# A two-layer encoder trunk on one core: the first mixer's attention rebuilt head by head

## The reference

```python
proj = x @ w_in
q, k, v, u = jnp.split(proj, ...)            # 8 query heads, 2 key/value heads of 64; u: 2 x 512 channels
q = apply_rope(rms_norm(q, q_norm_g), cos, sin)
k = apply_rope(rms_norm(k, k_norm_g), cos, sin)
# attention, each query head against all 512 keys of its group of 4
s = jnp.einsum('bqkgd,bskd->bkgqs', q_blk, k) * 64 ** -0.5
o = jnp.einsum('bkgqs,bskd->bqkgd', softmax(s), v)
# conformer convolution
a, gate = jnp.split(u, 2, axis=-1)
z = a * sigmoid(gate)                         # GLU, 512 channels
z = depthwise_conv(z, width 31) + dw_b        # over the tokens, per channel
conv = silu(layer_norm(z, norm_g, norm_b))    # norm over channels
m = concatenate([attn, conv]) @ w_out
```

## Time and profile before

| | us |
|---|---|
| median of 3 runs | 1436.73 (1434.38 to 1438.51) |
| the profiled execution | 1434.18 |
| its span | 1432.4 |
| PE busy in the span | 1383.2 (97%) |
| DVE busy | 664.6 (46%) |
| ACT busy | 459.6 (32%) |
| POOL busy | 221.6 (15%) |
| start of the output projection of layer 0 | 224.42 |

### The profile page before, as it was taken

One profiled execution on the slowest core, in us unless ns is written; L12 is line 12 of the kernel. 1 busy time (PEld: TensorE's weight loads), 2 busy tenths in 40 slices (PEclk: granted clock), 3 DMA queues, 4 the chain that ended last, 5 costly groups with the idle time before them and its releaser, 6 DMA issues.

```text
span 1432.4 us, 16564 instructions
## 1 busy us (share of the span) xinstructions
PE 1383.2 (97%) x6684; PEld 1162.5 (81%) x6684; DVE 664.6 (46%) x823; ACT 459.6 (32%) x552; POOL 221.6 (15%) x194
## 2 busy tenths in 40 slices
PE   7969789999999999999999999999999999999997
PEld 7757677888888888889888888888888888888886
DVE  4669893733333322166555453654373333332225
ACT  3357553332232221133232332423233222322211
POOL 5279851300000000033201002000030000000000
PEclk9989999999999999999999999999999999999999
DMA  6200001223222332303231212222222233224221
GB/s 213 89 30 1 30 30 59 89 88 109 96 88 94 109 120 88 115 33 137 67 105 59 88 59 88 89 89 89 88 89 88 88 99 106 88 89 146 88 89 59
DMA packets 84015, 124.15 MB, mean 87 GB/s; under 512 B 2688, under 2 KB 61312, under 8 KB 83968
## 3 DMA queue, kind: packets, MB, share of 16 engines
q1 hardware_dynamic: 83968, 123.49, 25.7%
HBM read 121.39 MB, written 2.10 MB: 86 GB/s over the span
## 4 chain that ended last, share of the span: by engine, by line
PE 86%; DVE 6%; POOL 4%; ACT 2%; issue 1%; DMA 0%; POOLq 0%; DVEq 0%; SPq 0%; ACTq 0%
PE ps L1236 22%; PE ps L1238 22%; PE ps L1237 22%; PE ps L1312 19%; DVE acc L914 2%; POOL acc L501 2%; POOL w_lo L377 1%; PE ps L1249 1%; ACT w_hi L373 1%; DVE row_max L1000 1%; DVE probT_lo L1017 1%; PE ps L1522 0%; PE ps L1442 0%; DMA x_tok<-in_x 0%; DVE x_tok L1059 0%
## 5 line engine op out<-in xcount | busy, mean ns | idle before, releaser
L377 DVE TENSOR_TENSOR w_lo<-raw,w_hi 128x2048 fp32r<-128x2048 f32 x101 | 231.8, 2295 | 487.1 <-ACT w_hi L373 487.1
L1236 PE MATMUL ps<-xT_hi,w_hi 128*128 128x512 f32 (+1 forms) x992 | 366.6, 370 | 0.5 <-POOL w_lo L377 0.5
L1237 PE MATMUL ps<-xT_lo,w_hi 128*128 128x512 f32 (+1 forms) x992 | 365.5, 368 | 0.0
L1238 PE MATMUL ps<-xT_hi,w_lo 128*128 128x512 f32 (+1 forms) x992 | 365.5, 368 | 0.0
L373 ACT ACTIVATE w_hi<-raw 128x2048 fp32r<-128x2048 f32 x109 | 208.4, 1912 | 429.7 <-PE ps L1238 251.1
L1236 PEld LDWEIGHTS ps<-xT_hi,w_hi 128*128 128x128 f32 x992 | 186.9, 188 | 32.1 <-POOL w_lo L377 1.1
L1238 PEld LDWEIGHTS ps<-xT_hi,w_lo 128*128 128x128 f32 x992 | 186.9, 188 | 31.4
L1237 PEld LDWEIGHTS ps<-xT_lo,w_hi 128*128 128x128 f32 x992 | 187.0, 188 | 31.2
L575 POOL TENSOR_SCALAR var_eps<-var_eps 128x1 f32<-128x1 f32 x16 | 5.6, 352 | 846.9 <-ACT squares L768 846.9
L1236 PE MATMUL ps<-w_hi,xT_hi 128*128 128x512 f32 (+1 forms) x320 | 121.3, 379 | 0.0
L1237 PE MATMUL ps<-w_lo,xT_hi 128*128 128x512 f32 (+1 forms) x320 | 121.1, 378 | 0.0
(11 more groups left out here) (167 smaller groups left out, 1760.8 us busy)
## 6 DMA issues: line engine op xcount, KB each, us to landing
raw<-in_l_w_in SPq DMA_DIRECT2D x31, 1024.0 KB, 5.2
raw<-in_l_ffn_w_gate SPq DMA_DIRECT2D x22, 1024.0 KB, 5.1
raw<-in_l_ffn_w_up SPq DMA_DIRECT2D x22, 1024.0 KB, 5.1
raw<-in_l_ffn_w_down SPq DMA_DIRECT2D x22, 1024.0 KB, 4.7
raw<-in_l_w_out SPq DMA_DIRECT2D x12, 1024.0 KB, 4.9
x_tok<-in_x SPq DMA_DIRECT2D x4, 512.0 KB, 7.2
out<-x_tok SPq DMA_DIRECT2D x8, 256.0 KB, 2.1
ln_gb<-in_l_ln_mix_g SPq DMA_DIRECT2D x2, 512.0 KB, 5.2
```

Of the source, the lines that this page charges most:

```text
L377: eng.tensor_tensor(w_lo[ch.s][:], raw[ch.s][:], f32(w_hi[ch.s][:]), ALU.subtract)\
L1236: nc.tensor.matmul(dst, a[0], b[0], start=start, stop=False)
L1237: nc.tensor.matmul(dst, a[0], b[1], start=False, stop=False)
L1238: return nc.tensor.matmul(dst, a[1], b[0], start=False, stop=stop)
```

## The change

- **Order of the head.** The first GLU pair is multiplied ahead of the queries: chunks are now KV, GLU 0 gate, GLU 0 value, Q, Q, GLU 1 gate, GLU 1 value, and each GLU pair is gate first.
- **Queries and keys.** The query is scaled by `q_scale` before it is turned and written twice side by side (`q_twice`, 1024 wide, line 998 of the new kernel, on DVE). After the turn, rows 0 to 63 hold its rounded part and rows 64 to 127 the rest (`q_pair`). The key stands twice and negated (`k_hi`, `k_lo`). One matmul over 128 rows thus does two parts, and the scores take two matmuls in place of three. They are the negative scores, and their row minimum is the exponential's shift: one DVE reduction (line 1020), with no `neg_max` behind it.
- **Order of the loop.** Step s is head s // 4, tile s % 4. The probabilities of one head are kept for all 512 queries, in two buffers.
- **Weighted values.** Once a head's four tiles are there, `weighted_values` issues 12 matmuls of 512 columns in one go (in steps 7, 11, ... 31 for the first seven heads, behind the last step for the eighth), with the output by feature. Two heads share a bank.
- **Division.** For a pair of heads POOL takes the inverse row sums and spreads them over 512 columns (`inv_wide`), PE turns them, ACT copies, DVE multiplies (`pair_scaled`) and takes the rest (`pair_lo`). `divide_outputs` and the turns of the output go.
- **Convolution.** All 31 taps of tile 3 are on PE, one each step (three matmuls). DVE has 46 taps in place of 49, 14 of them ahead of the loop, then one a step. POOL adds one a step.
- **Norm of the convolution.** It comes behind the loop. PE does the first two chunks' rows of token tiles 0 and 1 of the output projection in between (`first_rows`).

```diff
-C_Q = 1
-C_GLU = (3, 5)
+C_GLU = (1, 5)
+C_Q = 3
...
-            add_taps(18)
+            add_taps(7)
+            query_scale(0)
+            for t in range(1, TT):
+                add_taps(1)
+                query_scale(t)
...
+            add_taps(8)
...
             def attention_step(s):
-                b = s // 2
-                add_taps(1 + (s % 4 == 1))
+                b = s // 4
+                add_taps(1)
...
+            make_hi(act, Chunk(C_Q + 1))
+            tap_products(9)
             make_hi(act, Chunk(C_GLU[1]))
...
+            for t in range(TT):
+                query_square(t)
+                tap_products(1 + (t % 2))
             make_hi(act, Chunk(C_GLU[1] + 1))
-            glu_sigmoid(1)
-            tap_products(16)
+            tap_products(2)
             glu_sigmoid(2)
-            tap_products(4)
+            query_hi(0)
+            query_hi(1)
+            tap_products(2)
             glu_sigmoid(3)
...
-                mine(nc.vector.tensor_reduce(row_max[:, s:s + 1], ps[:, SCORE_BANKS[s % 2], :], AX.X, ALU.max))
-                nc.vector.tensor_scalar(neg_max[:, s:s + 1], row_max[:, s:s + 1], q_scale[:, t, h:h + 1], -1.0,
-                                        ALU.mult, ALU.mult).then_inc(max_made, 1)
...
+                nc.vector.tensor_reduce(neg_max[:, s:s + 1], ps[:, SCORE_BANKS[s % 2], :], AX.X, ALU.min).then_inc(max_made, 1)
...
-                conv(2 - s % 2)
...
+                conv(1)
+                if s >= 14 and s % 8 == 6 and s // 8 - 1 < PAIRS - 1:
+                    pair_scaled(s // 8 - 1)
+                if s >= 16 and s % 8 == 0 and s // 8 - 2 < PAIRS - 1:
+                    pair_lo(s // 8 - 2)
...
+                q, g = q_pair[:, t, h, :], h // (HEADS // KV)
+                nc.tensor.matmul(ps[:, SCORE_BANKS[s % 2], :], q, k_hi[:, g, :], start=True, stop=False)
+                nc.tensor.matmul(ps[:, SCORE_BANKS[s % 2], :], q, k_lo[:, g, :], start=False, stop=True).then_inc(scores_made, 1)
...
+                h, part = (s - 7) // TT, (s - 7) % TT
+                if 0 <= h < HEADS - 1 and part == 0:
+                    weighted_values(h, range(TT))
...
+            def weighted_values(h, key_tiles):
...
+                if 0 in key_tiles:
+                    pe.wait_ge(probT_lo_made, TT * (h + 1))
...
+                for k in key_tiles:
+                    v = v_parts[:, k, g].rearrange("p c d -> p (c d)")
+                    v_hi, v_lo = (v[:, HD * (c - odd):HD * (c - odd) + P] for c in (1, 3))
+                    last = product(out, (v_hi, v_lo), (probT_hi[:, b, k, :], probT_lo[:, b, k, :]),
+                                   not odd and k == 0, odd and k == TT - 1)
...
+            conv_to_tokens(0)
+            conv_to_tokens(1)
+            wait_split(pe, C_OUT0)
+            pe.wait_ge(att_lo_made, 2)
+            first_rows(0, 0)
+            conv_to_tokens(2)
+            pe.wait_ge(o_scaled, PAIRS - 1)
+            first_rows(0, 1)
+            conv_to_tokens(3)
+            wait_split(pe, C_OUT0 + 1)
+            pe.wait_ge(att_lo_made, PAIRS)
+            first_rows(1, 0)
+            first_rows(1, 1)
+            pe.wait_ge(conv_normed, TT)
+            for ct in range(CT):
+                conv_to_features(ct)
```

More of the change, by code:

```diff
@@ L407, in _ @@
                 sp.dma_start(dst, src).then_inc(par_landed, 16)
[L408 to L411, removed]
+            load(sp, Chunk(C_GLU[0] + 1), W0[:, :, A0:A0 + 256])
+            for j in range(2):
+                load(sp, Chunk(C_Q + j), W0[:, 4 * j:4 * j + 4, 0:512])
+            load_glu(1)
             for j in range(4):
@@ L553, in conv_rsqrt @@
                     .then_inc(conv_rstd, 1)
[L555 to L567, removed]
+            for s in range(LAST_STEP):
                 attention_step(s)
-            divide_outputs(STEPS // GROUP - 2)
-            conv_rsqrt(TT - 1)
-            divide_outputs(STEPS // GROUP - 1)
+            for t in range(TT):
+                conv_rsqrt(t)
             def norm_rstd(d, t):
@@ L1006, in _ @@
+            row_shift(0)
+            row_shift(1)
+            for n in range(TT, 2 * TT):
+                query_lo(n)
             glu_product(3)
@@ L1391, in glu_tiles @@
-            def glu_tiles(part, banks, between):
-                wait_split(pe, part)
-                feature_tiles(Chunk(part), banks, between)
-            glu_tiles(C_GLU[0], SIDE_B[0:2], lambda m: None)
-            pe.wait_ge(kT_lo_made, 4)
-            for t in range(2):
-                q_transposes(t)
-            glu_tiles(C_GLU[0] + 1, SIDE_B[2:4], lambda m: [q_transposes(t) for t in (2, 3)] if m else None)
-            glu_tiles(C_GLU[1], SIDE_B[0:2], lambda m: pe.wait_ge(z_made, m + 1))
@@ L1403, in attention_step @@
+            glu_tiles(C_GLU[1] + 1, VALUE_BANKS, inside_value)
             def attention_step(s):
@@ new lines, in _ @@
+            first_rows(0, 0)
[8 more added lines that the diff above has]
+            pe.wait_ge(conv_normed, TT)
+            for ct in range(CT):
+                conv_to_features(ct)
+            for t in (2, 3):
+                pe.wait_ge(silu_made, 2 * (t - 1))
+                last = first_rows(0, t)
@@ L1493, in swiglu @@
+            last.then_inc(chunk_used, 1)
+            for t in (2, 3):
+                last = first_rows(1, t)
+            last.then_inc(chunk_used, 1)
+            last_rows(C_OUT0, 4, (catT_hi, catT_lo), lambda row: pe.wait_ge(swish_lo_made, row - 3), 1)
             def swiglu(layer, c_ffn, c_down, stage):
```

562 lines of the change are left out of this document (301 added, 261 removed).

## The result

The changed kernel takes 1441.78 us (median of 6 runs, 1441.11 to 1443.21), the kernel before 1435.83 (6 runs): ratio 1.0041, 95% interval 1.0028 to 1.0054. It is slower by 0.4%, where 0.77% faster was forecast. The profiled execution took 1441.26 us.

The account below looks back on a forecast made before the run. DVE was taken to pace the loop, behind an 11 us hole on PE. Head -2.4, loop -8.7, tail 0 gave -11.1: span 1421.3, execution 1423, median 1425.6 us; own range 1418 to 1431, eight in ten 1415 to 1441.

Parts of the forecast that it names:

- that one moment: Mixer's end, where the output projection begins, 224.42 us before; gains were summed up to there, everything behind taken as unchanged.
- The loop: 29 steps, from step 2's reduction to step 31's: 93 us, 8.7 less than 101.7; range 87 to 106.
- I add 5 us: Loop: allowance for four queues waiting for each other, about one earlier DVE stall of 4.53 us.
- The sum of the parts: Loop without coupling: 25 steps at 2.70 us (67.5), splits 6, pair scalings 4.2, last four steps 9.6; 87.3 us.
- the burst by itself should be hidden: Loop: a head's twelve weighted-value products take 2.74 us, the scores behind wanted about 1.3 us later than they come.
- rival 3: Slower, chance 0.15: PE's low clock makes bursts 5.2 us and loop steps 2.1 longer; ten such steps give 1447.
- The head: Up to step 2's reduction: at about 109 us, 2.4 earlier than before; range 8 earlier to 8 later.
- The tail: From step 31's reduction to the mixer's end: 11.3 us net against 11.4 before, so no change; range 3 either way.
- Reductions that wait for PE after each burst: Loop, sign of being wrong: every fourth step longer than the others by more than 1 us.
- The signs of being right: Reductions 2.7 us apart in steps 3 to 26, step 2's near 109, step 31's near 202, PE idle below 6 before the loop.
- its 92: Head, sign of being wrong: the third sigmoid later than 92 us; it was expected near 87.5.
- the bound of 0.9: Loop, sign of being wrong: PE's granted clock below 0.9 over tens of us.

Follow-up runs that it names:

- e1_pad: The changed kernel with 128 unused bytes ahead of `work`, so its tensors stand where they stood before: 1433.25 us, 0.9978 of the kernel before.
- e2_before_moved: The kernel before with `row_max` placed elsewhere, so `work` and all behind it lies 128 bytes lower: 1443.9 us, 1.0057 of the kernel before.
- e5_inverse_later: The changed kernel with the transposes of a pair's inverse row sums two steps later, behind the burst, and ACT's copy one step later: 1430.45 us.
- e6_filled: The changed kernel with 28 extra products on PE ahead of its wait for the inverse of the first and second pair: 1439.07 us.
- e11_diagonals_first: The changed kernel with 128 bytes ahead of `work`, inverse transposes two steps later, and POOL's first two diagonal blocks ahead of its first seven additions: 1419.12 us.
- e3_split_late: The changed kernel with POOL's two splits of output weights in steps 13 and 21 instead of 8 and 16: 1439.57 us.
- e8_before_256: The kernel before with `row_max` and `neg_max` placed elsewhere, so `work` lies 256 bytes lower: 1436.38 us, 0.9996 of the kernel before.

## Why the prediction was wrong, step by step

**The sum left out a term: 8 us.** "Behind it nothing is changed, so the sum is made for that one moment": the code behind wasn't changed, its operands' addresses were. 7.17 us behind the mixer and 0.9 in the output projection; e1_pad and e2_before_moved show it in both directions, 8.5 and 7.2 us by the medians. It is more than twice the 3.4 us that the rebuilt mixer gains without it, and it alone turns the change from faster to slower. It is not the whole error: with the address put back the time is 1433.25 us, still above the forecast's own range of 1418 to 1431.

**The loop: 98.78 us instead of 93.** The term "I add 5 us" for coupling failed: DVE waits 19.78 us for scores. A second error of the other sign hides most of that. The sum of the parts, 87.3 us, was too large, for DVE is busy only 77.07 us in the loop (third pair of numbers, the columns of the earlier trace rows); of the changed kernel and of e5_inverse_later:

```profile
111.00:209.78 98.78, 73.51 (x345) 55.23 (x346) 77.07 (x93) 61.11 (x128) 70.26 (x48) 0.90 0.06 22
```

```profile
112.50:199.10 86.60, 69.95 (x345) 52.96 (x346) 74.54 (x93) 61.22 (x128) 72.91 (x48) 0.98 0.07 25
```

I had priced nearly every step at 2.70 us, with a tap beside POOL. Where POOL neither adds nor splits beside it, a tap has 0.73 us (139.78) and reductions come 1.87 apart (steps 8 and 9, 12 and 13, 20 and 21). That e5_inverse_later, without most of the waits for the inverse, comes to 86.60 and so near to 87.3 is chance: its DVE is busy 74.54 us and waits 10.4 for scores.

What made the coupling large: I had listed the inverses and the splits as load on POOL (81.5 against 87 us) and not as a queue: the inverse stands behind a 4.53 us split in POOL's order, and PE's place for it is *ahead* of the burst and of the next scores. The step "the burst by itself should be hidden ... about 1.3 us later than they come" was right for a burst without a wait ahead: 1.40 us at 127.46, at the full clock.

**The low clock (rival 3)** did not come as described, on step after step. It came behind the two long waits for the inverse and cost 2.7 us there (e6_filled). In e5_inverse_later, with the same change of banks from step to step and PE's short waits still there, the granted clock (behind PE's count) stays at its upper level until 160 us:

```profile
106.50:143.00 36.50, 27.40 (x136) 1.00 0.07 19
143.00:160.00 17.00, 12.70 (x68) 1.00 0.06 23
```

The Trainium skill (TensorE: Matmul & The Clock Gate, A second HAM failure mode) tells of a kernel whose clock swings because it cycles through PSUM banks; these two rows, 53.5 us of such a loop at 1.00, show no swing. Later in the same loop the clock did fall once, near 177 us, behind the wait of 1.98 us shown above. What let it fall there and not behind the 1.95 us at 150.31 is open.

**The head: step 2 at 111.00, not 109.** The order of events was right, and ACT's first tap came at 48.66 us (48.5 forecast); two sizes were not. ACT and POOL:

```profile
89.48 0.72 ACT L650 ACTIVATE tap_part<-zpad,conv_par 128x512 f32<-128x512 f32 x1 [10.24 <-POOL acc L499]
...
91.52 0.58 ACT L661 ACTIVATE tmp<-ps 128x512 f32<-128x512 f32 x1
```

```profile
82.44 1.65 POOL L512 TENSOR_TENSOR q_scale<-q_ms,minus_half 128x8 f32<-128x8 f32 x1 [5.77 <-DVE q_ms L992]
84.06 3.17 POOL L526 TENSOR_TENSOR diag<-ident,conv_par 128x512 f32<-128x512 f32 x2
```

The fourth scale came at 82.44 (79 assumed), since DVE ahead of it took 2.20 and 2.17 us for each wide scaling (1.5 assumed) and waited 1.51 for ACT's rounding of a weight chunk; two diagonals took 3.17 (2.5 assumed). So the third sigmoid starts at 91.52 and not near 87.5; of these 4 us 2.0 arrive at step 2. e11_diagonals_first, in which step 2 comes 2.0 us earlier, shows that the two diagonals lie on that path.

**The tail: +3.2 instead of nothing.** 0.9 is the address. The rest is work of PE that I had not placed: behind step 31's scores stands the burst of head 6 (12 products, 209.90 to 212.68), ahead of the last turns, and an inverse with its own wait of 0.73. The last burst starts at 216.27, 6.5 us behind the reduction, where I had 3.6. I had divided the bursts evenly over the last four steps ("a quarter of a burst"), and the last steps have a whole one.

Added up: 8.1 address, 5.8 loop, 2.0 head, 2.3 tail are the 18.2 us between the span forecast, 1421.3, and the measured 1439.5. On the median it is 16.2 us (1425.6 against 1441.78): I had carried over the 2.55 us by which the kernel before's median lay above its profiled execution, and for the changed kernel these are 0.52.

**Two slips in reading the rows.** The waits of the earlier trace rows reach up to 290 us, and I used them to say that PE's 34.00 us in the stretch from 106.5 to 143 "is no full load". Only 2.4 us of these waits lie there (1.9 for `probT_lo`, 0.5 for the exponential), so PE was nearly full beside DVE; the hole has 11.1 and the time behind 143 us has 14.4. And from 48.5 to 78.79 are 30.3 us, not 29. Neither enters the sum.

**Signs named ahead.** "Reductions that wait for PE after each burst" was the right one to watch. The waits are 1.40 us at step 8, 7.71 at 12, 6.87 at 20, 0.35 at 24 and 3.45 at 28: long where the inverse comes with the burst (12, 20, 28), short or none where the burst is alone. The signs of being right failed: between 77 and 106.5 us PE stood for 7.7 us (5.6 for `q_twice`, 2.1 for `q_pair`) in place of under 6, and step 31's reduction came at 209.78 in place of 202. In the loop ACT waited for POOL in front of `tap_part` only once, 0.4 us. The third sigmoid stayed inside its 92; the clock of 106.5 to 143 was 0.87 and of 143 to 160 0.89, below the bound of 0.9.

## What to carry to other kernels

Before a change is called local, compare the addresses of everything that is placed behind it: a removed tensor of 128 bytes cost more than twice what the change earned. When an operation is put in a queue ahead of critical work, follow its producer's queue back to the longest instruction in it; load by load the sum looks fine. A wait on PE can be paid twice if a burst follows it, so turns and other small products that can wait belong behind the burst.

## What the runs showed of the hardware

- fp32r products of 128x128 by 512 start 0.231 us apart on average instead of 0.226 when the base of the stationary tensors is 128 bytes below a multiple of 256 (519 against 531 in 120 us, clock 1.00). The bases 0, 256 and 512 bytes below 132 KB were alike; no reason is shown.
- DVE's tap, 0.73 us at 139.78, took 4.82 at 133.84, beside POOL's 4.53 us split, and ended 0.5 us behind it. The Trainium skill (SBUF — State Buffer, SBUF: two separate sides) says that a DVE instruction with two SBUF inputs and a GpSimd instruction that reads SBUF exclude each other for the whole of the instruction; the trace agrees in this place.
- A wait of 2.39 us on PE was followed by a whole burst at 0.43 us a product (e3_split_late), one of 1.98 us by a burst most of which ran at 0.43, and one of 1.95 us by a burst at 0.23 (both e5_inverse_later); no wait, or one of 0.46 us with products ahead of it, by one at 0.23. The length of the wait alone does not tell which.
- The moment at which the mixer ends differs by up to 2.5 us between profiled executions of kernels whose medians are alike (277.33 in the kernel before, 279.81 in e8_before_256), so a single profile does not settle a us or two; the medians do.
